# Seven block products in place of eight in the down projection of two feed-forwards

## Chip, cores and metric

One core of a Trainium2 chip runs one program of three model blocks. The metric is device time in microseconds (us) of one execution; lower is better. All figures below are of that one core.

## The reference, cut to what matters

Two of the three blocks hold a feed-forward, with D_MODEL = 1024, D_FF = 4096 and 1024 tokens:

```python
h = h + jnp.square(jax.nn.relu(m @ w_up[i])) @ w_down[i]     # second block, m = rmsnorm(h, g_mlp[i])
x = x + jnp.square(jax.nn.relu(h @ w_mlp1[l])) @ w_mlp2[l]   # third block,  h = rmsnorm_3(x, norm_mlp_g[l])
```

The change is in the second product of each line, the **down projection** from 4096 to 1024 features. All data is float32. Everything else of the three blocks (recurrent mixers, attention, convolutions, gates, norms) is untouched.

## The kernel before, in words

Features lie on the 128 partitions and tokens along the free dimension, so a tile is 128 features by 1024 tokens. One function, `feed_forward` (line 3335), is called once in the second block and once in the third. D is 1024, DFF 4096, KD = 8 (tiles of D), H = 4, W2 = 512 (half of the tokens), C2 = 2.

**Precision.** Each float32 factor is split into a rounded high part, which ScalarE writes (`high`, line 3537, for weights; `high_y`, L3567, for the inner tiles), and a rounded low part, which VectorE makes by subtraction (`low`, L3681; `low_y`, L3719; `low_w`, L3726). Each 128x128 by 128x512 product is then three matmuls: high times high, low times high, high times low.

**Up projection.** The 32 inner tiles are made in 16 pairs. Pair 0 and 1 are plain (`multiply_plain`). Pairs 2 to 15 use the seven products of a fast 2x2 block multiplication: the input is held in seven combined blocks `x`, `x_hi` (J = 7 blocks of H = 4 tiles of 512 tokens), the weights of a pair arrive raw in `raw`, VectorE makes the combined weight blocks with four additions (`combine`, L3665 to L3675), and `multiply(q, j)` runs 4 x 3 = 12 matmuls for each of the seven blocks j, 84 for a pair (L3490). Three running sums are kept in PSUM: X (blocks 0, 2, 4, 6 add to it), Y (blocks 1, 3) and Z (block 5). X and Y are read between blocks. ScalarE copies X, Y, X and X out after blocks 0, 1, 2 and 6 (`read`, L3563), VectorE adds Y, X, Z after blocks 3, 4, 5 (`read`, L3700) and then squares and scales a tile (`shape`, L3713 and L3715). SP stores the finished tiles `made_out` to the DRAM tensor `inner` and loads the raw weights of the pair after next (`load_pair`, L3398) once low part 5 of the next pair is made.

**Down projection.** 32 steps m of 48 matmuls each (L3511): four groups g of eight inner tiles, and in each group eight output tiles f. A step multiplies eight weight tiles by eight inner tiles over both halves of the tokens, and VectorE adds the sum in `acc` to the residual `hid` (L3803). The inner tiles come back from DRAM into a ring of RING = 14 places in the storage of `x` (`load_y`, L3422), one tile at a time. The next group's tiles are loaded and split while the current group is multiplied, one or two per step. Weights are double-buffered halves of 256 KB (`load_w`, L3412). In the last group ScalarE squares each finished output tile (L3625) and GpSimd sums the squares (L3649) for the next norm.

**What sets the order.** Every engine runs one list, in the order in which the code writes it, and waits on counting semaphores. So a VectorE instruction that waits holds up all that is written behind it. SP issues all of these transfers, also in one list.

The lines that `multiply` waits by in the up projection before:

```python
if j == 2: pe.wait_ge(act_read, act_reads(q) + 1)
if j == 6: pe.wait_ge(dve_read, dve_reads(q) + 2)
```

Of the kernel before, what the change touches and what calls it, by code (L numbers as in the profile page):

```python
# [8 lines left out]
F32 = mybir.dt.float32  # L9
# [3325 lines left out]
def feed_forward(nc, dram, n, hid, gain, up, down, sums):  # L3335
# [4 lines left out]
    PAIRS, LAST = DFF // P // 2, DFF // P // 2 - 1  # L3340
    G, H, J, RING = KD, KD // 2, 7, 14
    PLAIN, SLOT = 2, (0, 5, 6, 3)
    TILES = DFF // P
    with Part(nc, "ff" + n, dram) as p:
# [8 lines left out]
        w_in = [[p.sem(f"w_in{s}{a}") for a in range(2)] for s in range(2)]  # L3353
        y_in = [p.sem(f"y_in{i}") for i in range(RING)]
        stored = [p.sem(f"stored{s}") for s in range(2)]
# [3 lines left out]
        (d_high, d_low, y_high, y_low, used, done, acc_free, squared, summed) = (p.sem(a) for a in (  # L3359
            "d_high", "d_low", "y_high", "y_low", "used", "done", "acc_free", "squared", "summed"))  # L3360
# [3 lines left out]
        up_view, down_view = (a.rearrange("(k p) c -> p k c", p=P) for a in (up, down))  # L3364
        kept = dram["inner"].rearrange("(f p) t -> p f t", p=P)
        line = lambda a: a[:, :, :, :].rearrange("p j h n -> p (j h n)")
        y, y_hi = (line(a).rearrange("p (i t) -> p i t", t=SEQ) for a in (x, x_hi))
        w, w_hi = (line(a)[:, 0:2 * KD * P].rearrange("p (s k c) -> p s k c", s=2, k=KD) for a in (wl, wh))
# [4 lines left out]
        t3 = square[:, :, :].rearrange("p s (h n) -> p (s h) n", n=W2)  # L3373
        products = lambda q: 4 * min(q, PLAIN) + J * max(q - PLAIN, 0)
        act_reads = lambda q: 2 * min(q, PLAIN) + 4 * max(q - PLAIN, 0)
# [4 lines left out]
        Y, Z = bank[:, 2, :], bank[:, 3, :]  # L3380
# [3 lines left out]
        def _(sp):  # L3384
            def load_pair(q):
                cols = q * 2 * P
# [10 lines left out]
                for a in range(2):  # L3397
                    sp.dma_start(raw[:, a * H:(a + 1) * H, :], up_view[:, a * H:(a + 1) * H, cols:cols + 2 * P]).then_inc(raw_in[a], 16)  # L3398

            def store(q, i):  # L3400
                sp.wait_ge(made, 2 * q + (1 if i == first_half(q) else 2))
                sp.dma_start(kept[:, 2 * q + i, :], made_out[:, q % 2, i, :]).then_inc(stored[q % 2], 16)

            def load_w(m):
                g, f, s = m // G, m % G, m % 2
                if m < 2:
                    sp.wait_ge(product, products(LAST) + 2 * m + 2)
                else:
                    sp.wait_ge(done, m - 1)
                for a in range(2):  # L3410
                    ks = slice(a * H, (a + 1) * H)
                    sp.dma_start(w[:, s, ks, :], down_view[:, g * G + a * H:g * G + (a + 1) * H, f * P:(f + 1) * P]).then_inc(w_in[s][a], 16)  # L3412

            def load_y(i):
                sp.wait_ge(stored[i // 2 % 2], 32 * (i // 4 + 1))
                if i < RING:
                    sp.wait_ge(product, products(LAST) + i // 2 + 1)
                elif (i - RING) % G == G - 1:
                    sp.wait_ge(done, i - RING + 1)
                else:  # L3420
                    sp.wait_ge(used, (i - RING) // G * (G - 1) + (i - RING) % G + 1)
                sp.dma_start(y[:, i % RING, :], kept[:, i, :]).then_inc(y_in[i % RING], 16)  # L3422
            load_pair(0)
            load_pair(1)
            for q in range(LAST):
                store(q, first_half(q))
                if q + 2 < PAIRS:
                    load_pair(q + 2)
                store(q, 1 - first_half(q))
            load_y(0)  # L3430
            load_y(1)
            load_w(0)
            for i in range(2, 6):
                load_y(i)
            load_w(1)
            for i in range(6, 10):
                load_y(i)
            store(LAST, 1)
            for i in range(10, RING):
                load_y(i)  # L3440
            store(LAST, 0)
            for m in range(2, TILES):
                load_w(m)
                if m % G == 0:
                    for i in range(m + RING - G, min(m + RING, TILES)):
                        load_y(i)

        @block.tensor
        def _(pe):
# [17 lines left out]
            def multiply(q, j):  # L3467
                pe.wait_ge(w_low, products(q) + j + 1)
                if j == 0:
                    pe.wait_ge(act_read, act_reads(q - 1))  # L3470
                if j == 1 and q == PLAIN:
                    pe.wait_ge(act_read, 3)
                if j == 1 and q > PLAIN:
                    pe.wait_ge(dve_read, dve_reads(q - 1) + 1)
                if j == 2:
                    pe.wait_ge(act_read, act_reads(q) + 1)
                if j == 3:
                    pe.wait_ge(act_read, act_reads(q) + 2)
                if j == 4:
                    pe.wait_ge(act_read, act_reads(q) + 3)  # L3480
                if j == 5 and q > PLAIN:
                    pe.wait_ge(dve_read, dve_reads(q))
                if j == 6:
                    pe.wait_ge(dve_read, dve_reads(q) + 2)
# [751 lines left out]
```

## Time and profile before

| what | value |
|---|---|
| median of 3 runs | 4556.9 us |
| lowest, highest | 4551.75, 4563.9 us |
| span of the profiled execution | 4558.5 us |
| TensorE busy | 4230.4 us, 93% |
| VectorE busy | 2131.5 us, 47% |
| ScalarE busy | 1612.7 us, 35% |
| GpSimd busy | 446.8 us, 10% |
| DMA | 284.99 MB, mean 63 GB/s |

The profiled execution is told by its span, from its first to its last instruction; no other time of that execution is recorded. The span is 1.6 us above the median of the runs and inside their range. A matmul's busy time includes its overlap with its neighbours, so a busy TensorE still says only that the stream has no gaps; the length of a stretch and its number of matmuls give the pace.

### The profile page before, as it was taken

The numbers are of one execution on the slowest core, as the hardware profiler recorded it, in microseconds if no ns is written. First come the engines' busy times: TensorE is split into PE (matmuls) and PEld (weight loads), VectorE is DVE, ScalarE is ACT, GpSimd is POOL, SyncE is SP. The second block draws the span as 40 slices with busy tenths as digits, with TensorE's granted clock in tenths as the row PEclk, the third lists the DMA queues.
The fourth block names the chain that finished last, engine by engine and source line by source line (L and its number), as shares of the span: only waits on it lengthen the run. The fifth ranks groups of instructions, "written<-read, shape, count | busy, mean of one in ns | idle before, by whom it ended". The sixth has DMA issues, their size and how long they took to land. (4 is left out here: it accounts for less than half of the span.)

```text
span 4558.5 us, 66246 instructions
## 1 busy us (share of the span) xinstructions
PE 4230.4 (93%) x28112; PEld 3461.0 (76%) x28112; DVE 2131.5 (47%) x2980; ACT 1612.7 (35%) x2710; POOL 446.8 (10%) x378
## 2 busy tenths in 40 slices
PE   9988899988989979899998999999989888999998
PEld 8988889766978858677435788888767677888887
DVE  5645426364445551333443577433442364776333
ACT  5722234343423331311675433222332333433211
POOL 0034300010011100020231000001100001000001
PEclk9999999998999989999999999999999999999999
DMA  4110022222100021111001232421111221234232
GB/s 121 43 53 2 2 57 64 57 67 93 45 20 10 7 89 47 62 40 47 28 10 33 79 111 105 159 84 60 50 34 40 66 53 37 102 111 162 83 97 70
DMA packets 327271, 284.99 MB, mean 63 GB/s; under 512 B 16529, under 2 KB 293425, under 8 KB 326850
## 3 DMA queue, kind: packets, MB, share of 16 engines
q1 hardware_dynamic: 325682, 278.40, 19.7%
q8 instruction: 223, 3.65, 0.3%
q10 hardware_dynamic: 1296, 2.36, 0.2%
q14 instruction: 70, 0.57, 0.0%
HBM read 204.55 MB, written 55.31 MB: 57 GB/s over the span
## 5 line engine op out<-in xcount | busy, mean ns | idle before, releaser
L3511 PE MATMUL ff_acc<-ff_x_hi_rounded,ff_wh_rounded 128*128 128x512 f32 x1024 | 398.6, 389 | 0.0
L3511 PE MATMUL ff_acc<-ff_x_hi_rounded,ff_wl_rounded 128*128 128x512 f32 x1024 | 398.4, 389 | 0.0
L3511 PE MATMUL ff_acc<-ff_x_rounded,ff_wh_rounded 128*128 128x512 f32 x1024 | 398.4, 389 | 0.0
L3490 PE MATMUL ff_bank<-ff_x_hi_rounded,ff_wh_rounded 128*128 128x512 f32 x784 | 306.3, 391 | 5.7 <-issue 5.7
L3490 PE MATMUL ff_bank<-ff_x_rounded,ff_wh_rounded 128*128 128x512 f32 x784 | 306.3, 391 | 0.0
L3490 PE MATMUL ff_bank<-ff_x_hi_rounded,ff_wl_rounded 128*128 128x512 f32 x784 | 306.3, 391 | 0.0
L3573 ACT ACTIVATE ff_wh_rounded<-ff_wl 128x512 fp32r<-128x512 f32 x128 | 80.6, 632 | 407.4 <-DMA ff_wl<-w_mlp_dram 201.8
L3511 PEld LDWEIGHTS ff_acc<-ff_x_hi_rounded,ff_wh_rounded 128*128 128x128 f32 x1024 | 192.2, 188 | 40.6 <-DVE ff_x_rounded L3719 0.8
L3511 PEld LDWEIGHTS ff_acc<-ff_x_rounded,ff_wh_rounded 128*128 128x128 f32 x1024 | 192.2, 188 | 40.1
L3511 PEld LDWEIGHTS ff_acc<-ff_x_hi_rounded,ff_wl_rounded 128*128 128x128 f32 x1024 | 192.2, 188 | 39.7
L3803 DVE TENSOR_TENSOR all_hid<-all_hid,ff_acc 128x1024 f32<-128x1024 f32 x64 | 78.1, 1221 | 294.4 <-PE ff_acc L3511 294.4
L2306 PE MATMUL mid_acc<-b1h_hn_hi_rounded,mid_w_hi_rounded 128*128 128x336 f32 (+1 forms) x528 | 185.5, 351 | 6.1 <-DVE mid_w_rounded L2286 6.1
L2306 PE MATMUL mid_acc<-b1h_hn_hi_rounded,mid_w_rounded 128*128 128x336 f32 (+1 forms) x528 | 183.6, 348 | 0.0
L2306 PE MATMUL mid_acc<-b1h_hn_rounded,mid_w_hi_rounded 128*128 128x336 f32 (+1 forms) x528 | 183.3, 347 | 0.0
L3490 PEld LDWEIGHTS ff_bank<-ff_x_hi_rounded,ff_wh_rounded 128*128 128x128 f32 x784 | 148.0, 189 | 37.4 <-issue 6.5
L3490 PEld LDWEIGHTS ff_bank<-ff_x_rounded,ff_wh_rounded 128*128 128x128 f32 x784 | 147.9, 189 | 30.9
L3490 PEld LDWEIGHTS ff_bank<-ff_x_hi_rounded,ff_wl_rounded 128*128 128x128 f32 x784 | 147.8, 189 | 30.6
L3726 DVE TENSOR_TENSOR ff_wl_rounded<-ff_wl,ff_wh_rounded 128x512 fp32r<-128x512 f32 x128 | 99.0, 782 | 142.8 <-ACT ff_wh_rounded L3573 140.6
L2306 PE MATMUL pa_acc<-b1h_hn_hi_rounded,pa_w_hi_rounded 128*128 128x352 f32 (+1 forms) x432 | 145.9, 338 | 4.0 <-DVE b1h_w_first_rounded L2286 4.0
L2306 PE MATMUL pb_acc<-b1h_hn_hi_rounded,pb_w_hi_rounded 128*128 128x352 f32 (+1 forms) x408 | 135.9, 333 | 7.9 <-DVE b1h_w_first_b_rounded L2286 7.9
L2306 PE MATMUL pa_acc<-b1h_hn_rounded,pa_w_hi_rounded 128*128 128x352 f32 (+1 forms) x432 | 139.8, 324 | 0.0
L2306 PE MATMUL pb_acc<-b1h_hn_rounded,pb_w_hi_rounded 128*128 128x352 f32 (+1 forms) x408 | 131.7, 323 | 0.0
(704 smaller groups left out, 10445.5 us busy)
## 6 DMA issues: line engine op xcount, KB each, us to landing
inner<-ff_made_out SPq DMA_DIRECT2D x64, 512.0 KB, 2.6
ff_x<-inner SPq DMA_DIRECT2D x64, 512.0 KB, 5.4
ff_wl<-w_down_dram SPq DMA_DIRECT2D x64, 256.0 KB, 3.0
ff_wl<-w_mlp_dram SPq DMA_DIRECT2D x64, 256.0 KB, 3.1
ff_raw<-w_up_dram SPq DMA_DIRECT2D x30, 512.0 KB, 4.5
ff_raw<-w_mlp_dram SPq DMA_DIRECT2D x30, 512.0 KB, 4.2
mid_w<-w_in_dram SPq DMA_DIRECT2D x104, 128.0 KB, 2.6
p1o_w<-w_out_dram SPq DMA_DIRECT2D x32, 256.0 KB, 3.8
```

The source lines that it names most:

```text
L2306: mm = self.nc.tensor.matmul(self.acc[s][:, c, skip:width], rounded(l[:, k, :]), rounded(r[:, k, at]), start=(k == 0 and j == 0), stop=(k ...
L3490: mm = M(to, rounded(a[:, j, h, :]), rounded(b[:, j, h, :]), start=(j in (0, 1, 5) and h == 0 and i == 0), stop=(h == H - 1 and i == 2), s ...
L3511: mm = M(acc[:, s, c, :], rounded(a[:, s, k, :]), rounded(b[:, at, c * W2:(c + 1) * W2]), start=(k == 0 and i == 0), stop=(k == KD - 1 and ...
L3573: A(rounded(w_hi[:, s, a * H:(a + 1) * H, :]), w[:, s, a * H:(a + 1) * H, :], ACT.Copy).then_inc(d_high, 1)
L3726: T(rounded(w[:, s, part, :]), w[:, s, part, :], rounded(w_hi[:, s, part, :]), ALU.subtract).then_inc(d_low, 1)
L3803: T(cut(hid[:, f, :]), cut(hid[:, f, :]), acc[:, s, :, :], ALU.add).then_inc(acc_free, 1)
```

## The change

The down projection is computed as 16 further pairs with the up projection's seven products: pairs q = UPS = 16 to 31, in GROUPS = 4 groups of OUTS = 4 pairs. A group takes the eight inner tiles 8g to 8g+7 as a 2x2 block matrix (even and odd tiles, first and second half of the tokens), a pair gives two output tiles.

- The inner matrix needs seven blocks of four tiles by 512 tokens: three are the stored tiles themselves, four are **differences**. GpSimd makes the differences in the up projection with four 128x512 subtractions for each up pair (`difference`), into `differ` (the storage of `square`). SP stores them, 1 MB per pair, in a new DRAM tensor `inner_differences`. The stored even tiles shrink to their first half.
- At the last pair of each group, and at up pair 15 for group 0, SP loads the seven blocks of the next group (`load_y(g, j)`, 1 MB each), each as soon as the product that last used its place is done. ScalarE and VectorE make each block's high and low halves in two instructions of 1024 columns each. The raw weights of the pair after next go between block 5 and block 6 in SP's list.
- VectorE combines the weights as in the up projection (`combine`), and after each of the seven products adds the running sum to `hid` (`add`, seven instructions of 512 columns). `multiply` waits for these additions: block 2 for addition 0, block 3 for 1, block 4 for 2, block 6 for 4.
- Y and Z of down pairs lie in `acc`, double-buffered by pair.
- The last addition to `sums` goes to VectorE.

The diff, cut to its core:

```diff
-    PAIRS, LAST = DFF // P // 2, DFF // P // 2 - 1
+    UPS, GROUPS, OUTS = DFF // P // 2, DFF // D, D // P // 2
+    PAIRS, H, J = UPS + GROUPS * OUTS, KD // 2, 7
...
+        ends_group = lambda q: q >= UPS - 1 and (q + 1 - UPS) % OUTS == 0 and q + 1 < PAIRS
...
+            def load_y(g, j):
+                if j == 0:
+                    for s in range(2):
+                        sp.wait_ge(stored[s], 32 * H // 2 * (g + 1))
+                    sp.wait_ge(differences_stored, 16 * H * (g + 1))
+                sp.wait_ge(product, products(UPS - 1 + OUTS * g) + j + 1)
...
+                sp.dma_start(x[:, j], what).then_inc(y_in[j], 16)
             load_pair(0)
             load_pair(1)
+            for q in range(PAIRS):
+                if ends_group(q):
+                    for j in range(J - 1):
+                        load_y(group_of(q + 1), j)
+                        if q < UPS and j == 3:
+                            store_differences(q - 1)
+                elif 1 <= q < UPS or q == UPS + 1:
+                    store_differences(min(q, UPS) - 1)
+                if q < UPS - 1:
+                    store(q, first_half(q))
                 if q + 2 < PAIRS:
                     load_pair(q + 2)
+                if q < UPS - 1:
+                    store(q, 1 - first_half(q))
+                if q == UPS:
+                    store(q - 1, 1)
+                    store(q - 1, 0)
+                if ends_group(q):
+                    load_y(group_of(q + 1), J - 1)
...
+                if j == 0 and q >= UPS + 2:
+                    pe.wait_ge(added, adds(q - 1))
+                if q >= UPS and j in (2, 3, 4, 6):
+                    pe.wait_ge(added, adds(q) + {2: 1, 3: 2, 4: 3, 6: 5}[j])
...
+                    if q >= UPS and (q - UPS) % OUTS == 0 and h % 2 == 0:
+                        pe.wait_ge(y_low, 2 * (J * group_of(q) + j) + h // 2 + 1)
...
-            for m in range(TILES):
...
+            for q in range(PLAIN, PAIRS):          # ScalarE
                 for j in range(J):
+                    if q < UPS and j in (0, 1, 2, 6):
                         read(q, j)
+                    if q + 1 < PAIRS:
+                        high(q + 1, j)
+                    if ends_group(q) and j >= 1:
+                        high_y(group_of(q + 1), j - 1)
...
+                if ends_group(q):
+                    high_y(group_of(q + 1), J - 1)
...
+            def difference(q):
+                b11, b12, b21, b22 = part_of(q, 0, 0), part_of(q, 0, 1), part_of(q, 1, 0), part_of(q, 1, 1)
+                pool.wait_ge(made, 2 * q + 2)
+                if q == 0:
+                    pool.wait_ge(t_low, 4)
+                else:
+                    pool.wait_ge(differences_stored, 16 * q)
+                T(differ[:, 0], b12, b11, ALU.subtract).then_inc(differences, 1)
+                T(differ[:, 1], b22, b12, ALU.subtract).then_inc(differences, 1)
+                pool.wait_ge(differences, 4 * q + 1)
+                T(differ[:, 2], b22, differ[:, 0], ALU.subtract).then_inc(differences, 1)
+                pool.wait_ge(differences, 4 * q + 3)
+                T(differ[:, 3], b21, differ[:, 2], ALU.subtract).then_inc(differences, 1)
...
+            for q in range(UPS, PAIRS):
+                for j in range(J):
+                    if q == UPS and j == 0:
+                        low_y(0, 5)
+                    if q == UPS and j == 1:
+                        low_y(0, 6)
+                    add(q, j)
+                    if q + 1 < PAIRS:
+                        low(q + 1, j)
+                        if j < 2:
+                            combine(q + 1, j + 1)
+                    if ends_group(q) and j >= 1:
+                        low_y(group_of(q + 1), j - 1)
+                if q == UPS:
+                    shape(UPS - 1, 1)
+                    shape(UPS - 1, 0)
+                if ends_group(q):
+                    low_y(group_of(q + 1), J - 1)
```

At up pair 15 VectorE's list has `low_y(0, 0)` to `low_y(0, 4)` behind `low(16, 1)`, `low(16, 2)`, `low(16, 3)`, `low(16, 4)` and `low(16, 5)`, with `read(15, 3)` to `read(15, 5)` between them.

## Rows read from the trace of the kernel before

**Rows 1.** The page, its first lines and part 1.
```profile
span 4558.5 us, 66246 instructions
...
PE 4230.4 (93%) x28112; PEld 3461.0 (76%) x28112; DVE 2131.5 (47%) x2980; ACT 1612.7 (35%) x2710; POOL 446.8 (10%) x378
```

**Rows 2.** Busy time by stretch: both down projections (from:to, length, busy us and instructions of each engine, clock, DMA share, GB/s).
```profile
2859.80:3208.00 348.20, 348.20 (x1536) 287.98 (x1535) 126.09 (x127) 72.99 (x97) 15.43 (x7) 1.00 0.27 87
4180.00:4528.00 348.00, 348.00 (x1536) 287.93 (x1535) 125.62 (x127) 72.89 (x97) 15.42 (x7) 1.00 0.27 87
```

**Rows 3.** The same view: one pair of the up projection.
```profile
2807.35:2826.39 19.04, 19.04 (x86) 15.77 (x85) 14.19 (x20) 6.71 (x11) 0.00 (x0) 1.00 0.31 112
```

**Rows 4.** VectorE's instructions in that pair, in order of time.
```profile
2808.66 0.69 DVE L3665 TENSOR_TENSOR ff_wl<-ff_raw 128x512 f32<-128x512 f32 x1 [0.62 <-PE ff_bank L3490]
2809.39 0.69 DVE L3667 TENSOR_TENSOR ff_raw<-ff_raw 128x512 f32<-128x512 f32 x1
...
2816.72 0.69 DVE L3700 TENSOR_TENSOR ff_made_out<-ff_made_out,ff_bank 128x512 f32<-128x512 f32 x1 [1.36 <-PE ff_bank L3490]
2817.45 1.23 DVE L3713 SCALAR_TENSOR_TENSOR ff_made_out<-ff_made_out 128x1024 f32<-128x1024 f32 x1
...
2820.45 0.68 DVE L3700 TENSOR_TENSOR ff_made_out<-ff_made_out,ff_bank 128x512 f32<-128x512 f32 x1
2821.05 0.69 DVE L3681 TENSOR_TENSOR ff_wl_rounded<-ff_raw,ff_wh_rounded 128x512 fp32r<-128x512 f32 x1
```

**Rows 5.** ScalarE's instructions, the same pair and the first feed-forward's turn to down.
```profile
2806.69 0.63 ACT L3537 ACTIVATE ff_wh_rounded<-ff_raw 128x512 fp32r<-128x512 f32 x1 [0.24 <-DMA ff_raw<-w_up_dram]
...
2850.60 1.06 ACT L3567 ACTIVATE ff_x_hi_rounded<-ff_x 128x1024 fp32r<-128x1024 f32 x1 [0.64 <-DMA ff_x<-inner]
2852.16 1.06 ACT L3567 ACTIVATE ff_x_hi_rounded<-ff_x 128x1024 fp32r<-128x1024 f32 x1 [0.50 <-DMA ff_x<-inner]
```

**Rows 6.** VectorE, low halves of five loaded inner tiles in a row.
```profile
2863.01 5.76 DVE L3719 TENSOR_TENSOR ff_x_rounded<-ff_x,ff_x_hi_rounded 128x1024 fp32r<-128x1024 f32 x5
```

**Rows 7.** SP's queue: issue of one pair's weights, and of the first inner tiles.
```profile
2802.72 0.94 SPq L3398 DMA_DIRECT2D ff_raw<-w_up_dram  x2
...
2845.89 1.15 SPq L3422 DMA_DIRECT2D ff_x<-inner  x2
```

**Rows 8.** Busy time by stretch: the burst of inner tiles.
```profile
2855.00:2865.00 10.00, 10.00 (x44) 7.96 (x44) 9.97 (x11) 7.08 (x8) 0.00 (x0) 1.00 1.05 407
```

**Rows 9.** GpSimd and VectorE beside it, end of the first down projection.
```profile
3178.49 2.40 POOL L3649 TENSOR_TENSOR all_sums<-all_sums,ff_square 128x1024 f32<-128x1024 f32 x1 [8.49 <-ACT ff_square L3625]
...
3179.52 1.92 DVE L3726 TENSOR_TENSOR ff_wl_rounded<-ff_wl,ff_wh_rounded 128x512 fp32r<-128x512 f32 x1 [2.20 <-ACT ff_wh_rounded L3573]
```

**Rows 10.** GpSimd and VectorE beside it, in the attention stage.
```profile
2291.66 1.27 POOL L3096 TENSOR_TENSOR stick_run<-stick_run,stick_soft 128x512 f32<-128x512 f32 x1 [2.07 <-PE stick_score L3019]
...
2292.42 0.69 DVE L3112 SCALAR_TENSOR_TENSOR stick_soft<-stick_score,stick_soft 128x512 f32<-128x512 f32 x1 [1.12 <-ACT stick_soft L3066]
```

**Rows 11.** TensorE behind its one wait in the first up projection.
```profile
2599.95 0.56 PE L3490 MATMUL ff_bank<-ff_x_hi_rounded,ff_wh_rounded 128*128 128x512 f32 x1 [3.46 <-issue]
2600.31 0.63 PE L3490 MATMUL ff_bank<-ff_x_hi_rounded,ff_wl_rounded 128*128 128x512 f32 x1
```

**Rows 12.** Busy time by stretch: the 19 us around that wait.
```profile
2588.00:2607.00 19.00, 15.54 (x62) 12.40 (x61) 9.74 (x14) 8.15 (x13) 0.00 (x0) 0.91 0.28 84
```

**Rows 13.** The load that this wait hangs on, and its reader.
```profile
2593.58 0.94 SPq L3398 DMA_DIRECT2D ff_raw<-w_up_dram  x2
...
2598.74 0.63 ACT L3537 ACTIVATE ff_wh_rounded<-ff_raw 128x512 fp32r<-128x512 f32 x1 [5.68 <-DMA ff_raw<-w_up_dram]
```

**Rows 14.** The tail of the first down projection, in order of time.
```profile
3208.74 1.22 DVE L3803 TENSOR_TENSOR all_hid<-all_hid,ff_acc 128x1024 f32<-128x1024 f32 x1 [9.66 <-PE ff_acc L3511]
3209.99 1.06 ACT L3625 ACTIVATE ff_square<-all_hid 128x1024 f32<-128x1024 f32 x1 [9.82 <-DVE all_hid L3803]
3211.12 2.34 POOL L3649 TENSOR_TENSOR all_sums<-all_sums,ff_square 128x1024 f32<-128x1024 f32 x1 [8.48 <-ACT ff_square L3625]
```

More of the change, by code:

```diff
@@ L3363, in feed_forward @@
         block = p.stack.enter_context(nc.Block())
[L3364 to L3368, printed above, removed]
+        up_view = up.rearrange("(k p) c -> p k c", p=P)
+        down_view = down.rearrange("(q i p) c -> i p q c", i=2, p=P)
+        kept = dram["inner"].rearrange("(q i p) t -> i p q t", i=2, p=P)
+        kept_differences = dram["inner_differences"].rearrange("q d p n -> d p q n")
         cut = lambda a: a.rearrange("p (c n) -> p c n", c=C2)
@@ L3766, in _ @@
                 low(PLAIN, j)
-            for q in range(PLAIN, LAST):
+            for q in range(PLAIN, UPS):
+                last = q == UPS - 1
                 for j in range(3):
@@ L3771, in _ @@
                         combine(q + 1, j + 1)
+                    if last and j >= 1:
+                        low_y(0, j - 1)
                 read(q, 3)
                 low(q + 1, 3)
+                if last:
+                    low_y(0, 2)
                 read(q, 4)
-                shape(q, 1)
+                if not last:
+                    shape(q, 1)
                 low(q + 1, 4)
+                if last:
+                    low_y(0, 3)
                 read(q, 5)
                 low(q + 1, 5)
+                if last:
+                    low_y(0, 4)
@@ L3779, in _ @@
                 low(q + 1, 6)
-                shape(q, 0)
-            read(LAST, 3)
-            read(LAST, 4)
-            low_y(0)
-            low_y(1)
-            low_w(0)
-            read(LAST, 5)
-            low_y(2)
-            shape(LAST, 1)
-            for i in range(3, KD):
-                low_y(i)
-            low_w(1)
-            shape(LAST, 0)
-            for m in range(TILES):
-                g, f, s = m // G, m % G, m % 2
-                if g >= 1 and f == 0:
-                    low_y(m + 6)
-                    low_y(m + 7)
-                if 2 <= m + 1 < TILES:
-                    low_w(m + 1)
-                if g + 1 < TILES // G and f < 6:
-                    low_y(m + G)
-                dve.wait_ge(done, m + 1)
-                T(cut(hid[:, f, :]), cut(hid[:, f, :]), acc[:, s, :, :], ALU.add).then_inc(acc_free, 1)
+                if not last:
+                    shape(q, 0)
```

217 lines of the change are left out of this document (84 added, 133 removed).

## The prediction

> **What bounds the kernel now.** I read the page first: TensorE is busy 93% of a span of 4558.5 us, every other engine under half [rows 1]. Then the busy time by stretch for the two down projections: 1536 matmuls fill 348.2 us without a gap, at the full clock, so one costs 348.2 / 1536 = 0.2267 us [rows 2]. An up pair takes 19.04 us for 84 matmuls, the same 0.2267 [rows 3]. In a down projection VectorE works 126 of 348 us, in an up pair 14.2 of 19.04 [rows 2, 3]. So TensorE sets both stages, a removed matmul is worth its 0.2267 us only while the others keep up, and a block j of 12 matmuls, 2.72 us, is the beat on which they must.
>
> **What is removed.** Each down projection goes from 1536 to 16 x 84 = 1344 matmuls: 192 x 0.2267 = 43.5 us, 87.0 for both. The tail shrinks too: today 1.22 us on VectorE, 1.06 on ScalarE, 2.34 on GpSimd follow the last matmul [rows 14], 4.8 us with the gaps; then it is an addition of half the size (0.7), a square of 1.06 and an addition of 1.22 on VectorE, 3.0 us. Gain 1.8 each, **3.6** in all. Sum of the gains: 90.6 us.
>
> **Within a group: nothing.** A down pair asks of VectorE seven additions, seven low parts and four combinations. Started back to back such instructions come every 0.60 us, behind a wait every 0.73 [rows 4]: about 12 of 19 us. The closest place: combination 1 starts once block 1 is done, two of them take 1.4, addition 1 another 0.65, and block 3 waits for it with 2.7 us to go. Some 0.4 us is left. Addition 2 has the same. I take 0; the cover is that 0.4, and if a wake-up costs more, up to 0.3 us a pair, 10 us in all.
>
> **At each turn of a group the list of VectorE is too long.** The last pair of a group carries, besides the 12 us, 14 low halves of 1024 columns. Five in a row took 5.76, so 1.15 each [rows 6]: 16.1 us. That is 28 us of work in a pair of 19, and the additions that TensorE waits for stand in the same list. I follow the list from the start of that pair, with additions and low parts at 0.62, combinations at 0.70, halves at 1.15, and done blocks seen 0.2 us after their end. A block of the inner matrix is 1 MB. The nearest rows for its transfer: two loads issued at 2845.89 reached ScalarE at 2850.60 and 2852.16, so 1 MB took up to 6.2 us; a first half of a weight pair issued at 2802.72 was read at 2806.69, 3.9 us after 0.5 MB [rows 5, 7]. In the burst the DMA moved 407 GB/s [rows 8], so each further MB queued adds 2.6. I take 5.5 for one, with 3.9 and 6.2 as ends.
> - Low half 0 ends at 12.1, addition 2 at 12.7: block 4 starts at 12.8 in place of 10.9. Lost 1.9.
> - Halves 1 and 2 end at 19.2, addition 4 at 19.8: block 6 starts at 19.9 in place of 18.3. Lost 1.7.
> - Halves 3 end at 22.8, low part 5 at 24.0. Only now SP may issue the raw weights and, behind them, block 6 of the inner matrix, at 25.0. It lands behind 1 MB of weights at 32.3; ScalarE needs 1.06 for each half [rows 5]. VectorE would be through with half 5 at 29.9, waits, ends half 6 at 35.7, and addition 0 of the new group at 36.3. Block 2 starts at 36.4 in place of 28.1. Lost 8.3.
>
> Sum 11.9 us, three times for each feed-forward: 35.7. If block 6 came at once, the third term would be 4.7 and the sum 8.3; with the slow ends 12.9.
>
> **The turn from up to down** has the same 14 halves, and in addition GpSimd's differences of pair 14. What GpSimd does to VectorE: a sum of 1024 columns ran from 3178.49 to 3180.89, and a VectorE low part started at 3179.52 took 1.92 instead of 0.69 [rows 9, 4]; it stood until GpSimd had finished. An instruction that reads PSUM beside SBUF took 0.69 under a running GpSimd instruction [rows 10]. So low parts, combinations and halves wait for GpSimd, additions from PSUM don't. A 128x512 subtraction of GpSimd takes 1.2 (half of 2.40) to 1.27 [rows 9, 10]; four make 4.8 to 5.1 us. By the list, with the two engines taking turns, the second read of pair 15 ends at 22.8: its last block starts at 22.9 in place of 16.3, lost 6.6. Block 6 of the inner matrix is issued at 28.0 behind raw weights, lands at 35.2, ScalarE splits it ahead of its next weight tile, and block 3 of pair 16 starts at 43.0 in place of 35.6, lost 7.4. The `shape` instructions of pair 15 (four of 1.2) and its differences fall into pair 17 and delay additions 0, 1 and 2 by 1.6, 3.0 and 0.5. Together 19.1 us per feed-forward; without GpSimd's part 16, with late landings 21.
>
> **The clock.** After a gap of 3.46 us TensorE's instructions started 0.36 to 0.43 us apart, not 0.2267: the lower of its two levels, 1.2 against 2.4 GHz [rows 11]. Over the 19 us around it the granted clock was 0.91 [rows 12], so a gap of that size costs a further 0.09 x 19 = 1.7 us. Five gaps of each feed-forward are longer (three of 8.3, one of 4.0, the second part of the 6.6, and one of 7.4): 5 x 1.75 = 8.8 us.
>
> **The start and the up pairs.** GpSimd's differences of pair 0 run while VectorE makes the low parts of pair 2, and SP now stores them before it issues pair 3. Today that load is issued at 2593.58 and ScalarE waits for it until 2598.74, which is TensorE's gap [rows 13, 11]; each us by which low part 5 is later is lost. One or two turns of 1.2: I take 2 us per feed-forward, between 0 and 5. In the 13 later up pairs VectorE's 14.2 us and GpSimd's 4.8 to 5.1 add to 19.0 to 19.3 against 19.04 [rows 3]. I take 1.5 us in all for each feed-forward, as 1.9 us of VectorE's work reads PSUM and can run beside GpSimd; the bounds are 0 and 6. The added stores (1 MB a pair, in a stage at 112 GB/s of 407 [rows 3, 8]) and ScalarE's added waits for the differences of two pairs back cost nothing: their cover is that room, and a whole pair of time.
>
> **Sum.** Per feed-forward lost: 35.7 + 19.1 + 8.8 + 2 + 1.5 = 67.1 us; gained 43.5 + 1.8 = 45.3. Net 21.8 slower, 43.6 for both: 4558.5 + 43.6 = 4602.1 by the profiled span. The median of the runs is 1.6 lower, so the forecast is **4600 us**, 0.95% slower. With all terms at their low ends (8.3 x 3, 16, 5, 0, 0 = 45.9) the two sides all but cancel: 4560. With all at their high ends (12.9 x 3, 21, 9, 5, 6, and 5 within groups = 84.7) it is 4558.5 + 78.8 = 4637.
>
> **Rivals.**
> - *The turns are absorbed, faster.* If the low halves were to hold TensorE only at the first block of a new group (4.7 us, with no clock lost), and 8 us at the turn from up to down, the loss would be 22 and the gain 45: 4558.5 - 46 = **4512**. For it: VectorE idles over 60% of the down projection before [rows 2]. Against: the additions stand in the same list behind the halves, and that idle time lies in other pairs. It would need halves of 0.6 us, and the rows show 1.15 [rows 6]. Chance 0.12.
> - *Level.* Low ends of most terms, above all no lower clock after the gaps: 4545 to 4570, around **4557**. For it: the gaps may be split in ways that keep the clock up. Against: a gap of 3.46 was enough once [rows 11]. Chance 0.16.
> - *The up projection becomes bound by the pair VectorE and GpSimd.* If each change of turn costs time, or a subtraction takes 1.5 us, the cycle of an up pair is 14.2 + 6.0 = 20.2, and 13 pairs in two feed-forwards lose 30 us: 4600 + 24 = **4624** to 4650. For it: the sum of the two is at 19.0 to 19.3 already. Against: reads from PSUM overlap [rows 10]. Chance 0.17. The Trainium skill (SBUF — State Buffer, section Who interferes with whom) says that a VectorE instruction with two SBUF inputs and a GpSimd instruction that reads SBUF exclude each other for a whole instruction, in both directions. By that rule an up pair cannot be under 14.2 + 5.0 less the 1.9 of PSUM reads; the trace agrees for VectorE, which waited 1.2 us [rows 9], and no row here shows how long GpSimd waits.
> - *The differences are not ready or a wait orders things otherwise.* The first load of a group waits for stores of pairs at least four back for groups 1 to 3 only in name, as those stores are issued at pair 17 at the latest. I see no case in which it holds. No chance of its own.
>
> **How the numbers follow.** A measurement of this kernel can tell about 0.3% from no change, 14 us. The forecast's case (4575 to 4635) has 0.55, the port rival 0.17: slower 0.72. Level 0.16, faster 0.12. The range for 8 in 10 goes from 4550, which takes in most of the level case, to 4645, which takes in the high ends and most of the port rival.
>
> **What would show it.** In the changed profile: about 27700 matmuls; down pairs of 19.0 us inside a group, with VectorE some 12 busy; TensorE's waits named on the VectorE `add` line, three gaps of 8 us in each down projection 76 us and more apart, and on ScalarE's or VectorE's reads in up pair 15; a granted clock under 1 behind each. GpSimd's subtractions at 1.2 to 1.3, VectorE's low parts in up pairs at more than 0.69 on average. The forecast is wrong if the gap at a group's start is under 5 us, if the up pairs are not 19.1 us within 0.2, or if the inner blocks land in under 4 us.

## The result and the profile after

The changed kernel takes 4605.07 us (median of four runs, 4603.96 to 4626.57) against 4554.93 us (four runs, 4551.75 to 4563.9): a ratio of 1.0119, 95% interval 1.0097 to 1.0142. The profiled execution took 4603.96 us, with a span of 4602.2 against 4558.5 [rows 1]. The same comparison for one feed-forward at a time, from the first matmul that totals the squares of its norm (`ff_acc<-all_sums`) to the same matmul of the next norm: 675.1 and 673.7 us before, 693.8 and 697.5 after. The sum of the two, 1348.8 and 1391.3, is called the **stage sum** below (it is 42.5 us up); it leaves out the rest of the program, whose length differs by some us between profiled executions.

The top of the page of the changed kernel, which answers to [rows 1]:

```profile
span 4602.2 us, 66798 instructions
...
PE 4171.3 (91%) x27728; PEld 3401.3 (74%) x27728; DVE 2483.3 (54%) x3414; ACT 1715.5 (37%) x2854; POOL 641.7 (14%) x504
```

TensorE is 59 us less busy and the span 44 longer, so some 100 us more are idle. The waits of TensorE show where. In the first feed-forward, 2540 to 3190 (total us, times, longest):

```profile
PE ff_bank L3492 <- issue: 30.1, 4, 8.2
PE ff_bank L3492 <- DVE all_hid L3723: 10.4, 7, 1.8
PE ff_acc L3492 <- issue: 6.7, 1, 6.7
...
PE ff_bank L3492 <- DVE ff_made_out L3693: 3.6, 1, 3.6
```

L3723 is `add`. Where "issue" stands, the row shows only which instruction was late; what held it is in VectorE's list. One turn between groups, TensorE's instructions behind a gap (start, duration, in brackets the idle time before and its releaser):

```profile
2955.19 0.47 PE L3492 MATMUL ff_bank<-ff_x_hi_rounded,ff_wh_rounded 128*128 128x512 f32 x1 [1.75 <-DVE all_hid L3723]
...
2962.13 0.47 PE L3492 MATMUL ff_bank<-ff_x_hi_rounded,ff_wh_rounded 128*128 128x512 f32 x1 [1.21 <-DVE all_hid L3723]
...
2978.73 0.77 PE L3492 MATMUL ff_bank<-ff_x_hi_rounded,ff_wh_rounded 128*128 128x512 f32 x1 [8.17 <-issue]
2979.30 0.63 PE L3492 MATMUL ff_bank<-ff_x_hi_rounded,ff_wl_rounded 128*128 128x512 f32 x1
```

The same three gaps, in front of block 4, block 6 and block 2 of the new group, come at every turn. The third is 7.45 to 8.17 us. Behind it the instructions start 0.43 us apart: TensorE is at the lower of its two clocks. VectorE's list at that turn, one issue of SP's and one row of ScalarE's show why:

```profile
2961.30 0.68 DVE L3723 TENSOR_TENSOR all_hid<-all_hid,ff_bank 128x512 f32<-128x512 f32 x1
...
2962.50 2.36 DVE L3714 TENSOR_TENSOR ff_x_rounded<-ff_x,ff_x_hi_rounded 128x1024 fp32r<-128x1024 f32 x2
...
2969.44 2.36 DVE L3714 TENSOR_TENSOR ff_x_rounded<-ff_x,ff_x_hi_rounded 128x1024 fp32r<-128x1024 f32 x2
2975.67 2.36 DVE L3714 TENSOR_TENSOR ff_x_rounded<-ff_x,ff_x_hi_rounded 128x1024 fp32r<-128x1024 f32 x2 [3.88 <-ACT ff_x_hi_rounded L3554]
2977.95 0.68 DVE L3723 TENSOR_TENSOR all_hid<-all_hid,ff_bank 128x512 f32<-128x512 f32 x1
```

```profile
2967.05 0.51 SPq L3424 DMA_DIRECT2D ff_x<-inner  x1
```

```profile
2974.58 2.00 ACT L3554 ACTIVATE ff_x_hi_rounded<-ff_x 128x1024 fp32r<-128x1024 f32 x2 [6.59 <-DMA ff_x<-inner]
```

A pair of low halves (L3714) takes 2.4 us; seven pairs of them stand among the additions. The last pair waits 3.88 us for block 6, which was issued at 2967.05 behind the raw weights and reached ScalarE 7.5 us later. Only behind it stands addition 0 of the new group (2977.95), for which TensorE waits.

Four stretches of the changed kernel (length; busy time and count of PE, PEld, DVE, ACT, POOL; granted clock, DMA share, GB/s): the up pairs from the start's gap to the turn to down (thirteen pairs and that turn's first gap), a stretch inside group 0, one turn to the next, and the start of the lower clock behind a gap.

```profile
2604.00:2860.00 256.00, 254.25 (x1113) 210.08 (x1114) 231.75 (x242) 90.05 (x150) 82.33 (x52) 0.99 0.44 160
2912.00:2955.00 43.00, 41.33 (x180) 33.63 (x180) 28.89 (x43) 12.96 (x19) 0.45 (x1) 1.00 0.42 145
2955.19:3045.59 90.40, 79.27 (x337) 64.27 (x337) 62.86 (x87) 31.26 (x43) 0.00 (x0) 0.94 0.37 129
2979.30:2983.20 3.90, 3.90 (x11) 3.04 (x10) 2.42 (x4) 0.63 (x1) 0.00 (x0) 0.50 0.00 0
```

From turn to turn it is 90.4 us, where four pairs of 19.04 [rows 3] would be 76.2. Inside a group nothing is lost: from 2912.07 to the idle time before 2955.19 it is 41.4 us for 180 matmuls, where 180 x 0.2267 is 40.8. At the turn from up to down, and in the pair after:

```profile
2857.94 0.47 PE L3492 MATMUL ff_bank<-ff_x_hi_rounded,ff_wh_rounded 128*128 128x512 f32 x1 [1.75 <-ACT ff_made_out L3549]
...
2867.29 0.76 PE L3492 MATMUL ff_bank<-ff_x_hi_rounded,ff_wh_rounded 128*128 128x512 f32 x1 [3.63 <-DVE ff_made_out L3693]
...
2886.70 0.76 PE L3492 MATMUL ff_acc<-ff_x_hi_rounded,ff_wh_rounded 128*128 128x512 f32 x1 [6.68 <-issue]
...
2906.79 0.47 PE L3492 MATMUL ff_bank<-ff_x_hi_rounded,ff_wh_rounded 128*128 128x512 f32 x1 [1.49 <-DVE all_hid L3723]
...
2912.07 0.47 PE L3492 MATMUL ff_acc<-ff_x_hi_rounded,ff_wh_rounded 128*128 128x512 f32 x1 [2.28 <-DVE all_hid L3723]
```

### The profile page after: what moved, and what is told of

Same layout as the page of the kernel before. It is cut to its first block and busy times, and to the rows that moved or that the text cites. A ratio compares the mean times of both kernels' runs of the same rounds, so it can differ in the third digit from the quotient of the medians.

```text
span 4602.2 us, 66798 instructions
## 1 busy us (share of the span) xinstructions
PE 4171.3 (91%) x27728; PEld 3401.3 (74%) x27728; DVE 2483.3 (54%) x3414; ACT 1715.5 (37%) x2854; POOL 641.7 (14%) x504
## 5 line engine op out<-in xcount | busy, mean ns | idle before, releaser
L3492 PE MATMUL ff_bank<-ff_x_hi_rounded,ff_wh_rounded 128*128 128x512 f32 x1296 | 515.3, 398 | 92.2 <-issue 59.8
L3492 PE MATMUL ff_bank<-ff_x_hi_rounded,ff_wl_rounded 128*128 128x512 f32 x1296 | 511.6, 395 | 0.0
L3492 PE MATMUL ff_bank<-ff_x_rounded,ff_wh_rounded 128*128 128x512 f32 x1296 | 511.1, 394 | 0.0
L3522 ACT ACTIVATE ff_wh_rounded<-ff_raw 128x512 fp32r<-128x512 f32 x240 | 151.0, 631 | 288.9 <-PE ff_bank L3492 141.7
L3674 DVE TENSOR_TENSOR ff_wl_rounded<-ff_raw,ff_wh_rounded 128x512 fp32r<-128x512 f32 x240 | 183.4, 766 | 46.6 <-ACT ff_wh_rounded L3522 46.0
L3492 PE MATMUL ff_acc<-ff_x_hi_rounded,ff_wh_rounded 128*128 128x512 f32 x384 | 151.8, 395 | 19.8 <-issue 15.2
L3492 PE MATMUL ff_acc<-ff_x_hi_rounded,ff_wl_rounded 128*128 128x512 f32 x384 | 150.9, 393 | 0.0
L3492 PE MATMUL ff_acc<-ff_x_rounded,ff_wh_rounded 128*128 128x512 f32 x384 | 150.6, 392 | 0.0
L3723 DVE TENSOR_TENSOR all_hid<-all_hid,ff_bank 128x512 f32<-128x512 f32 x128 | 87.7, 685 | 104.5 <-PE ff_bank L3492 104.5
L3714 DVE TENSOR_TENSOR ff_x_rounded<-ff_x,ff_x_hi_rounded 128x1024 fp32r<-128x1024 f32 x112 | 131.9, 1220 | 21.6 <-ACT ff_x_hi_rounded L3554 21.6
L3554 ACT ACTIVATE ff_x_hi_rounded<-ff_x 128x1024 fp32r<-128x1024 f32 x112 | 112.5, 1052 | 78.9 <-DMA ff_x<-inner 57.2
```

Source lines behind the costliest of these rows:

```text
L3492: mm = M(to, rounded(a[:, j, h, :]), rounded(b[:, j, h, :]), start=(j in (0, 1, 5) and h == 0 and i == 0), stop=(h == H - 1 and i == 2), s ...
L3522: A(rounded(wh[:, j]), source[j], ACT.Copy).then_inc(w_high, 1)
L3554: A(rounded(x_hi[:, j, 2 * a:2 * a + 2]), x[:, j, 2 * a:2 * a + 2], ACT.Copy).then_inc(y_high, 1)
L3674: T(rounded(wl[:, j]), source[j], rounded(wh[:, j]), ALU.subtract).then_inc(w_low, 1)
L3714: T(rounded(x[:, j, part]), x[:, j, part], rounded(x_hi[:, j, part]), ALU.subtract).then_inc(y_low, 1)
L3723: T(to, to, what, ALU.add).then_inc(added, 1)
```

## The experiments

All start from the changed kernel; the last three build on the one before, as said there. Each batch ran beside the kernel before; the stage sum is from each kernel's own profile.

| run | median us | ratio to before (95%) | stage sum us |
|---|---|---|---|
| before | 4554.9 to 4557.4 | 1 | 1348.8 |
| the change | 4605.07 | 1.0119 (1.0097 to 1.0142) | 1391.3 |
| no_differences | 4586.1 | 1.0060 (1.0039 to 1.0080) | 1374.9 |
| block6_first | 4581.3 | 1.0042 (1.0023 to 1.0060) | 1367.8 |
| thin_lows | 4578.1 | 1.0035 (1.0013 to 1.0057) | 1370.1 |
| filler | 4591.62 | 1.0082 (1.0058 to 1.0106) | 1380.6 |
| thin_lows_6 | 4554.71 | 0.9990 (0.9980 to 0.9999) | 1350.2 |
| sums_first | 4558.54 | 1.0010 (0.9998 to 1.0022) | 1343.4 |
| sums_first_6 | 4573.79 | 1.0030 (1.0010 to 1.0050) | 1350.6 |
| all_turns | 4525.51 | 0.9947 (0.9922 to 0.9971) | 1318.6 |
| all_turns_2 | 4501.75 | 0.9882 (0.9861 to 0.9902) | 1291.8 |

**no_differences: GpSimd's part.**

```diff
-                T(differ[:, 0], b12, b11, ALU.subtract).then_inc(differences, 1)
+                T(differ[:, 0, 0:1], b12[:, 0:1], b11[:, 0:1], ALU.subtract).then_inc(differences, 1)
...
+            nc.gpsimd.memset(differ, 0.0).then_inc(cleared, 1)
```

> Leaves out GpSimd's work: each of the four subtractions per up pair is one column wide, on storage cleared once; stores, loads and waits stay. So the differences are not computed. Theory (VectorE's list at the turns of the groups is too long, GpSimd's use of the shared reads costs only at the start and at the turn from up to down): the three gaps at inner turns (1.75, 1.2 and 7.5 to 8.2 us) stay; the gap in the first up pairs (6.7 and 6.4 us) goes back to 3 to 4, and the turn from up to down loses 3 to 6 us less. Sum 6 to 9 us for each feed-forward: 4588 to 4594 us. Rival, the port: what VectorE and GpSimd do to each other is most of the 50 us lost, and the time falls below 4570. Rival, the DMA: nothing changes, 4603 to 4607.

Measured: 4586.1, and 16.4 us less in the stage sum. Its gaps from the start to the first turn between groups:

```profile
2597.22 0.47 PE L3492 MATMUL ff_bank<-ff_x_hi_rounded,ff_wh_rounded 128*128 128x512 f32 x1 [2.67 <-issue]
...
2879.18 0.77 PE L3492 MATMUL ff_acc<-ff_x_hi_rounded,ff_wh_rounded 128*128 128x512 f32 x1 [5.18 <-issue]
...
2968.37 0.77 PE L3492 MATMUL ff_bank<-ff_x_hi_rounded,ff_wh_rounded 128*128 128x512 f32 x1 [7.53 <-issue]
```

The gap at the start is 4.1 and 3.1 us shorter in the two feed-forwards (2.67 and 3.30 against 6.74 and 6.36), the gaps of the turn from up to down are 2.8 and 3.6 us shorter in all; the turns between groups, where no GpSimd work runs, keep their 1.75, 1.24 and 7.5 to 8.3 (once 4.08 in place of the first two). So GpSimd costs 8 us per feed-forward, nearly all at the beginning and the end of its own work, and the cause of the larger part is elsewhere.

**block6_first: the late block.** At the turns between groups SP issues block 6 ahead of the weights.

```diff
+                if ends_group(q) and q >= UPS:
+                    load_y(group_of(q + 1), J - 1)
...
-                if ends_group(q):
+                if ends_group(q) and q < UPS:
```

> At the three inner turns SP issues block 6 of the inner matrix before the raw weights of the pair after next; VectorE's and ScalarE's lists are untouched. Theory: block 6 is issued at the end of the last product, some 2.5 us earlier, and no longer behind 1 MB of weights; VectorE gets through with its halves 3 to 4 us earlier, and the gap before block 2 of a new group falls from 7.5 to 8.2 us to 4 to 5. Six of them: 4580 to 4586 us. Rival, only the amount of VectorE's work counts: no change, 4605. Rival, TensorE now waits for the weights that were put behind: the gap stays as long and moves to another block.

Measured: 4581.3, and a third gap of 4.19 to 4.23 us, as expected. Now VectorE's list has no wait in it and alone sets the gap:

```profile
2969.31 4.62 DVE L3716 TENSOR_TENSOR ff_x_rounded<-ff_x,ff_x_hi_rounded 128x1024 fp32r<-128x1024 f32 x4
2973.85 0.67 DVE L3725 TENSOR_TENSOR all_hid<-all_hid,ff_bank 128x512 f32<-128x512 f32 x1
```

**thin_lows: less VectorE work at the turns.** The low halves of groups 1 to 3 are made for 64 of 512 columns only, and the third matmul of each product reads the high part in their place.

```diff
-                    for i, (a, b) in enumerate(((wh, x_hi), (wl, x_hi), (wh, x))):
+                    for i, (a, b) in enumerate(((wh, x_hi), (wl, x_hi), (wh, x if q < UPS + OUTS else x_hi))):
...
+                        T(rounded(x[:, j, part, 0:64]), x[:, j, part, 0:64], rounded(x_hi[:, j, part, 0:64]), ALU.subtract).then_inc(y_low, 1)
```

> Leaves out most of the low halves of the inner matrix in groups 1 to 3: 64 columns per tile are made in place of 512, and the third matmul of each triple reads the high part in place of the low one; loads, ScalarE's halves, waits and counts of matmuls stay. Theory: VectorE's share of each inner turn falls from 28 to 16 us, the first two gaps (1.75 and 1.2) go, and of the third only what the transfer and ScalarE's halves of block 6 set is left, 3 to 5 us; per turn 8 us less, six turns 48: 4552 to 4562 us. Rival, transfers and ScalarE set the turns, not VectorE: the gaps keep more than 6 us and the time stays above 4590.

**This missed**, by 16 us: 4578.1. In the first feed-forward the gaps before blocks 4 and 6 are gone but for one of 1.2 and two under 0.4, yet the third is still 6.6 to 7.2 us (5.8 to 7.1 in the second), where I had left 3 to 5. ScalarE's row for block 6, issued at 2958.84, shows the cause:

```profile
2966.97 2.00 ACT L3554 ACTIVATE ff_x_hi_rounded<-ff_x 128x1024 fp32r<-128x1024 f32 x2 [5.40 <-DMA ff_x<-inner]
```

The transfers of the turn ran at 329 to 393 GB/s, near the burst of [rows 8], from 2945 to 2965; one stretch of the four:

```profile
2950.00:2955.00 5.00, 5.00 (x23) 3.95 (x23) 3.40 (x8) 4.48 (x6) 0.00 (x0) 1.00 1.05 393
```

Thin halves let the list run ahead, and then block 6 alone holds the same addition 0. Two causes lie side by side: the list alone gives 4.2 us (block6_first), the transfer alone 6.8 in the mean, both 7.8.

**thin_lows_6: both edits.**

> Both edits at once: low halves of groups 1 to 3 mostly left out (64 of 512 columns made, the third matmul of each triple reads the high part) and block 6 of the inner matrix issued before the raw weights. Theory: two things hold block 2 of a new group at about the same time, VectorE's list and the late block 6, and taking either away leaves the other (4.2 us behind block6_first, 6.6 to 7.2 us behind thin_lows). With both away the gap falls to 2 to 3.5 us, what one transfer of 5.2 us, two halves of ScalarE and an addition take beyond two blocks: 4545 to 4558 us. Rival, ScalarE's list (18.5 us of work in a pair of 19) is the third bound: the gap stays above 4 us, 4562 or more.

Measured: 4554.71, inside the expectation, with one gap of 2.8 to 3.9 us at each turn and, once, one of 1.4 ahead of it. Together the edits take 41.1 us off the stage sum; alone they take 21.2 (thin_lows) and 23.5 (block6_first), 44.7 in all.

**filler: the clock.** 28 extra matmuls into an unused PSUM bank run in the third gap of each turn.

```diff
+                if q > UPS and (q - UPS) % OUTS == 0 and j == 2:
+                    pe.wait_ge(y_low, 2 * (J * group_of(q) + 2) + 1)
+                    for i in range(FILL):
+                        M(bank[:, 2, :], rounded(wh[:, 2, 0, :]), rounded(x_hi[:, 2, 0, :]), start=True, stop=True, skip_group_check=True)
```

> Before block 2 of groups 1 to 3 TensorE runs 28 further matmuls into an unused bank of PSUM (6.3 us at the full clock), which lie in the gap of 7.5 to 8.2 us before that block. Theory: the gap is filled, the clock keeps its upper level, and the matmuls behind it start 0.227 us apart from the first; 1.7 us less at each of six turns: 4593 to 4597 us. Rival, the lower clock behind a gap costs nothing because VectorE's list is late anyway: 4605. If the fillers outlast the gap: slower, by under 1 us each.

Measured: 4591.62, and 10.7 us less in the stage sum, 1.8 for each of six turns. The gap is down to 1.0 to 1.5 us, and the block starts hardly earlier (0.2 us in the mean). The 19 us from that start on, at the first turn of filler and then at the second of the changed kernel (columns as in the stretches above):

```profile
2975.10:2994.10 19.00, 19.00 (x84) 15.74 (x85) 12.39 (x19) 4.43 (x7) 0.00 (x0) 1.00 0.17 56
```

```profile
3068.69:3087.69 19.00, 19.00 (x77) 15.62 (x78) 11.88 (x19) 4.44 (x7) 0.00 (x0) 0.91 0.18 56
```

84 matmuls in place of 77: seven of 0.2267 us, 1.6 us, are what the lower clock takes there. At the change's other turns it was 71 to 77.

**sums_first: the order alone.** VectorE does the same work at the turns between groups, but each addition comes as soon as it can, and the low halves of blocks 3 to 6 move into the new group's first pair, behind its addition 0, each ahead of the block that needs it.

```diff
+                if ends_group(q):
+                    g = group_of(q + 1)
...
+                    low_y(g, 0)
+                    add(q, 3)
+                    low(q + 1, 3)
+                    add(q, 4)
+                    low_y(g, 1)
...
+                if q > UPS and (q - UPS) % OUTS == 0:
+                    g = group_of(q)
+                    add(q, 0)
+                    low_y(g, 3)
+                    add(q, 1)
+                    low_y(g, 4)
...
```

> Nothing is left out and no work is removed: only VectorE's list at the three inner turns is written anew, so that the additions that TensorE waits for stand first, low halves 3 to 6 stand in the next pair, each just ahead of the block that needs it, and the weights of the pair after stand behind them. SP's and ScalarE's lists stay. Theory (it is the order of the list, not its length, that holds TensorE: 28 and 12 us of work fit almost in two pairs of 38): the gaps fall from 1.75, 1.2 and 7.5 to 8.2 us to a sum under 2 us, and the clock stays up; 10 to 12 us less per turn, six turns: 4530 to 4545 us. Rival, the amount of work counts: TensorE waits elsewhere in the two pairs for at least 5 us per turn, 4560 or more. Rival, block 6 comes too late behind the raw weights: a gap before block 6 of each new group.

Measured: 4558.54. The turns have no gap over 0.4 us and come every 81.3 to 82.4 us, against 89 to 91; but the expectation was missed by 13 us, since the next pair has new gaps:

```profile
2986.35 0.47 PE L3492 MATMUL ff_bank<-ff_x_hi_rounded,ff_wh_rounded 128*128 128x512 f32 x1 [0.69 <-DVE all_hid L3723]
...
2991.67 0.47 PE L3492 MATMUL ff_acc<-ff_x_hi_rounded,ff_wh_rounded 128*128 128x512 f32 x1 [2.35 <-DVE all_hid L3723]
```

In VectorE's list addition 1 (2990.84) stands behind two combinations:

```profile
2989.51 0.69 DVE L3658 TENSOR_TENSOR ff_wl<-ff_raw 128x512 f32<-128x512 f32 x1
2990.24 0.69 DVE L3660 TENSOR_TENSOR ff_raw<-ff_raw 128x512 f32<-128x512 f32 x1
2990.84 0.68 DVE L3723 TENSOR_TENSOR all_hid<-all_hid,ff_acc 128x512 f32<-128x512 f32 x1
```

**sums_first_6: the two orders together.** sums_first with the edit of block6_first.

> As sums_first, and SP issues block 6 of the inner matrix before the raw weights at inner turns. Theory: in the new order block 6 is needed some 8 us later than it lands, so its place in SP's list no longer matters: the same time as sums_first within 3 us. Rival, the transfer still ends the turn: 10 us or more below sums_first.

Measured: 4573.79, 15 us above sums_first, though the stage sums differ by 7 and the second feed-forwards by 0.6 (674.6 and 675.2). The gaps in front of the same blocks are as long, with one more of 1.9 us. What is longer in the first feed-forward are the starts behind them: behind gaps of 2.31, 2.48 and 2.33 us the granted clock was 0.91 or 0.92 over 19 us, where sums_first had 1.00 behind 2.29, 2.44 and 2.37. The scatter of its five runs, 24 us, doesn't let me say that it is slower; it shows only that an earlier block 6 brings nothing that can be seen once addition 0 doesn't stand behind it.

**all_turns: the same for the turn from up to down**, on top of sums_first_6, with ScalarE's high halves of that turn one step later, the shaping and storing of up pair 15 one pair later, and the weights of pair 3 issued before the first store of differences.

```diff
+                    if q == 1:
+                        load_pair(q + 2)
                     store_differences(min(q, UPS) - 1)
...
+                if q == UPS:
+                    add(q, 0)
+                    low_y(0, 2)
+                    add(q, 1)
+                    low(q, 6)
+                    low_y(0, 3)
+                    add(q, 2)
...
+                    if q == UPS + 1 and j in (3, 5):
+                        shape(UPS - 1, 1 if j == 3 else 0)
```

> As sums_first_6, and the same for the turn from up to down (reads of pair 15 before low halves, halves 2 to 6 in pair 16, each just ahead of its block; ScalarE's halves one step later, so that its copies of pair 15 are not behind a transfer; the two shape steps of pair 15 and its stores in pair 17), and at the start SP issues the weights of pair 3 before the first store of differences. Nothing is left out. Theory: the turn from up to down loses 20 us and a lowered clock now and then 4 to 8; the start 2 us less; some 15 us less than sums_first_6 for each feed-forward: 4500 to 4515 us, 1% below the kernel before. Rival, GpSimd's differences, which fall into the same pairs, keep the turn at 15 us or more: 4525 or more.

Measured: 4525.51, 10 us above what was expected. The gaps of 6.7, 3.6 and 1.75 at that turn are down to one of 0.2 and one of 0.4; the start is 4.12 in place of 6.74; the rest is the pair after each turn, up to 1.5 us before block 2 and 2.3 to 2.9 before block 3, as in sums_first. The time meets the rival's number, 4525 or more, but not its cause: the turn itself no longer holds TensorE for 15 us.

**all_turns_2: each addition one step earlier**, on top of all_turns. In the down pairs, all but the first of each group, the addition stands ahead of the combinations.

```diff
+                add(q, 0)
                 for j in range(J):
-                    add(q, j)
                     if q + 1 < PAIRS:
                         low(q + 1, j)
-                        if j < 2:
-                            combine(q + 1, j + 1)
+                    if j + 1 < J:
+                        add(q, j + 1)
+                    if q + 1 < PAIRS and j < 2:
+                        combine(q + 1, j + 1)
```

> As all_turns, and in VectorE's list of every down pair each addition stands one step earlier: addition j+1 ahead of the combinations of weights that stood before it. Nothing is left out. Behind all_turns TensorE still waited twice in the second pair of each group (0.5 to 1.5 us before block 2, 2.3 to 2.9 us before block 3), where VectorE is late from the turn and the combinations stood ahead of addition 1. Theory (order, not amount): both waits go or fall under 0.5 us together; four such pairs in each feed-forward, 8 to 13 us each: 4500 to 4510 us. Rival, VectorE simply has too much work in the three pairs around a turn: the wait moves to a weight's low part and the time stays at 4520 or more.

Measured: 4501.75, inside the expectation. That is 1.2% under the kernel before and 2.3% under the change (0.9882 / 1.0119), so it beats both. Its page and TensorE's waits in the first feed-forward:

```profile
span 4496.9 us, 66798 instructions
...
PE 4148.5 (92%) x27728; PEld 3382.4 (75%) x27728; DVE 2475.4 (55%) x3414; ACT 1705.4 (38%) x2854; POOL 642.4 (14%) x504
```

```profile
PE ff_bank L3494 <- DVE all_hid L3727: 4.9, 5, 1.5
PE ff_bank L3494 <- issue: 4.1, 1, 4.1
...
PE ff_acc L3494 <- DVE all_hid L3727: 4.0, 4, 1.1
```

The same 66798 instructions, and VectorE busy for 2475 us against 2483. Nothing was taken off any engine; the places in the lists, VectorE's above all and with it some of SP's and ScalarE's, are worth 99.5 us of stage sum. VectorE's list at the turns between groups alone is worth 47.9 of them (sums_first).

## Why the prediction was right, step by step

It forecast 4600 us; the profiled span was forecast at 4602.1 and was 4602.2. Such agreement is partly luck, since some terms were off against each other. In us for one feed-forward (the mean of the two):

| term | forecast | measured |
|---|---|---|
| gaps, three turns between groups | 35.7 | 32.6 |
| gaps, turn from up to down | 19.1 | 16.8 |
| gap at the start, over that of before | 2 | 3.7 |
| clock and up pairs | 10.3 | 13.4 (what is left) |
| gains | 45.3 | 45.3 (taken as forecast) |
| net | 21.8 | 21.2 |

- **A removed matmul is worth 0.2267 us while nothing waits.** Held: 27728 matmuls, and inside a group 180 of them took 41.4 us, where 40.8 was due. The term of nothing within a group was right too. The tail held too: the next norm's first matmul waited 4.04 us in place of 5.87 for its releaser, 1.8 less.
- **The turns between groups.** Sizes and places held: 1.9, 1.7 and 8.3 forecast, 1.75, 1.2 (once 2.0) and 7.5 to 8.2 measured. The landing of block 6 was forecast at 7.3 us and took 7.5; with block 6 early, 4.7 was forecast and 4.2 came. What the working missed is that the transfer alone would hold some 7 us even with the list empty: it credited the transfer only with the last 3.6. That is why thin_lows was misjudged.
- **The turn from up to down.** The forecast's gaps of 6.6, 7.4 and 1.6, 3.0, 0.5 were 5.4, 6.7, 1.5 and 2.3 in the first feed-forward, 5.4, 8.6, 1.5 and 2.3 in the second. GpSimd's share was forecast at 3; no_differences has 2.8 and 3.6 us less gap there.
- **The clock.** 1.75 a gap forecast, 1.8 by filler. The trace of the change has the rest of the 13.4 us, counted from start to start of its matmuls: behind the five long gaps they come 9.2 us late in the first feed-forward and 10.4 in the second, 2.0 a gap in the mean, against 0.2267 us apiece. Another 2.2 us stand in no idle time, as a gap is counted from the modelled end of the matmul before, 0.39 us after its start, and not from 0.2267: 0.16 for each of 14 further gaps. The last 1.4 are late starts behind short gaps and behind the start's.
- **The start was sized too small.** The step counted low part 5's delay alone, and that was well sized: the load of pair 3 was issued at 2596.03, counted from the feed-forward's first matmul 1.7 us later than before [rows 13]. What it left out is the landing, 6.7 us later in place of 5.2 (1.7 + 1.5 = 3.2, the added gap being 3.3), as the differences and a tile are stored ahead of the load:

```profile
2594.28 0.37 SPq L3413 DMA_DIRECT2D inner_differences<-ff_square  x1
2594.69 0.51 SPq L3409 DMA_DIRECT2D inner<-ff_made_out  x1
2596.03 1.73 SPq L3404 DMA_DIRECT2D ff_raw<-w_up_dram  x2
```

  In all_turns the weights go first: they are read 4.1 us after their issue, in place of 6.7, and the gap falls by the same 2.6 us, to 4.1.
- **The up pairs.** 1.5 us were set against the shared work of VectorE and GpSimd; it cost nothing: TensorE's list has no gap between 2603.92 and 2857.94, though VectorE is busy 231.75 of 256 us, 91% where it was 75% [rows 3].
- **The rivals.** Absorbed: no, the turns cost what the sum said. Level: no. The up projection bound by VectorE and GpSimd: no, a subtraction takes even more than the 1.5 us it feared (1.60 in the mean of the four), but TensorE waits nowhere in it. (Its time of 4624 adds 24 us where its own 30, less the 3 already in the sum, make 27; nothing hangs on it.) That the change would do something else: no.
- **What the prediction did not see.** It named VectorE's list as *too long*. Sums_first and all_turns_2 show that the amount of its work isn't the cause: with the same instructions, the halves of four blocks placed one pair later, the gaps at the turns go. Block 6's halves aren't needed until block 6 of the new pair; they held TensorE at block 2 only because addition 0 stood behind them.

**What stays open.** Why the lower clock comes behind some gaps of 2.2 to 3.3 us and not behind others; what each edit of all_turns is worth by itself; the 4.1 us left at the start; and how much faster all_turns_2 would be without its last gaps of 0.5 to 1.5 us, most of them in the pair after a turn.

## What to carry to other kernels

Where an engine off the bound feeds one that sets the time, order its list by when the consumer needs each result, and put what it frees first: here one order costs 1.2% and another gains as much, with the same instructions. Count the list per beat in the pair with the most work, not by its average; and before a load is credited with the last part of a stall, ask what it alone would hold if everything beside it were free. A smaller count of matmuls is worth its time only after that.

## What the hardware showed that was not expected

**VectorE and GpSimd take turns one instruction at a time.** Both engines' instructions in the first half of one up pair:

```profile
2697.35 1.28 POOL L3619 TENSOR_TENSOR ff_square<-ff_made_out 128x512 f32<-128x512 f32 x1 [12.65 <-DVE ff_made_out L3708]
...
2698.59 1.74 POOL L3620 TENSOR_TENSOR ff_square<-ff_made_out 128x512 f32<-128x512 f32 x1
2699.10 1.77 DVE L3658 TENSOR_TENSOR ff_wl<-ff_raw 128x512 f32<-128x512 f32 x1
2700.29 1.74 POOL L3622 TENSOR_TENSOR ff_square<-ff_made_out,ff_square 128x512 f32<-128x512 f32 x1
2700.91 1.67 DVE L3660 TENSOR_TENSOR ff_raw<-ff_raw 128x512 f32<-128x512 f32 x1
```

The first subtraction, which finds VectorE idle, takes 1.28 us, and a VectorE one alone 0.69; together both start every 1.7 to 1.8 us, so each waits for the other. The Trainium skill (SBUF — State Buffer, section Who interferes with whom) says that a VectorE instruction with two SBUF inputs contends with a GpSimd instruction that reads SBUF, and that this is an exclusive lock. The trace agrees; in the prediction only the VectorE side had a row. I had expected the subtractions at 1.2 to 1.3. The mean of the combinations over the up pairs (us in all, mean ns), 1.69 us where it was 0.69:

```profile
L3658 DVE TENSOR_TENSOR ff_wl<-ff_raw 128x512 f32<-128x512 f32 x12 | 20.3, 1693 | 0.8 <-PE ff_bank L3492 0.7
```

A VectorE instruction that reads PSUM beside SBUF is not held. In the up pairs these reads (L3693) don't test it, as none starts while a GpSimd instruction runs. In the down pairs 16 additions do, and take 0.67 to 0.69 us, such as this one in the last group:

```profile
3188.42 2.41 POOL L3639 TENSOR_TENSOR all_sums<-all_sums,ff_square 128x1024 f32<-128x1024 f32 x1 [11.19 <-ACT ff_square L3563]
```

```profile
3189.28 0.69 DVE L3723 TENSOR_TENSOR all_hid<-all_hid,ff_acc 128x512 f32<-128x512 f32 x1 [1.36 <-PE ff_acc L3492]
```

**Short gaps can lower the clock too.** In sums_first a gap of 2.35 us followed one of 0.69; some 1.2 us behind it TensorE's instructions went over to starts 0.42 us apart, and the granted clock over the next 19 us was 0.91:

```profile
2991.67:3010.67 19.00, 19.00 (x77) 15.52 (x78) 10.03 (x16) 3.80 (x6) 0.00 (x0) 0.91 0.18 56
3073.05:3092.05 19.00, 19.00 (x84) 15.72 (x85) 11.97 (x19) 4.43 (x7) 0.00 (x0) 1.00 0.17 56
```

The second row is the same place one group later, behind gaps of 0.45 and 2.44: there the clock stayed at 1.00, and 84 matmuls went in place of 77. So 2.4 us of gap came with the lower clock in one place and not in the other. Longer gaps did both, too. The prediction had a gap of 3.46 as its shortest example, but the kernel before has one of 2.25 (at 3920.04), behind which it was 0.91. At the start of no_differences it was 0.91 behind 2.67 us in the first feed-forward and 1.00 behind 3.30 in the second. At the turns of thin_lows_6 it was 0.91 behind five gaps of 2.8 to 3.9 us and 1.00 behind one of 3.02. The 19 us behind the 3.30 of no_differences:

```profile
3930.97:3949.97 19.00, 19.00 (x84) 15.75 (x85) 16.05 (x22) 7.12 (x12) 1.05 (x4) 1.00 0.52 194
```
